# A Mamba-2 and mixture-of-experts layer: second modulation on TensorE column groups, residue products last, scan heads in turn on two array halves

## What is computed

```python
mx = modulation(c, ada_w, ada_b)              # silu(c) @ w + b, six vectors of 2048
hx = modulate(rms_norm(x, g0), mx[0], mx[1])  # the same for ctx with c_ctx
yx = ssd_mixer(hx, hc, ...)                   # two-direction Mamba-2 scan, context first
x = x + mx[2] * yx
hx = modulate(rms_norm(x, g1), mx[3], mx[4])
y = hier_moe(hx, ...)                         # top-1 group, top-2 of its experts
x = x + mx[5] * y
```

## Time and profile before

| | |
|---|---|
| median of 3 runs | 2401.31 us (2399.72 to 2412.43) |
| profiled execution, its own time | 2409.67 us |
| its span (first to last instruction) | 2408.1 us |
| PE busy, DVE busy, ACT busy | 85%, 50%, 20% of the span |
| mean clock of TensorE | 0.94 of full speed |

### The profile page before, as it was taken

How to read it: one execution, slowest core, us unless ns; L and a number is a source line. 1 busy time by engine, 2 the same in 40 slices (tenths; PEclk the granted TensorE clock), 3 DMA queues, 4 the chain that set the end, 5 groups by cost and what they waited for, 6 DMA issues and landing times. The chain is left out here.

```text
span 2408.1 us, 27833 instructions
## 1 busy us (share of the span) xinstructions
PE 2048.1 (85%) x9989; PEld 1254.5 (52%) x9989; DVE 1196.3 (50%) x1865; ACT 490.8 (20%) x513; POOL 107.0 (4%) x148
## 2 busy tenths in 40 slices
PE   4678999999999999996699769888888888888887
PEld 2257777777777777775478553333333333333332
DVE  2256776777777777776354553222222222222223
ACT  3122333333323233332244320000000000000000
POOL 0000000000000000000370000000000000000000
PEclk8678999999999999998899869999999999999999
DMA  6967656565647474646355509999999999999997
GB/s 223 318 198 215 180 160 189 155 202 146 211 132 225 127 214 142 212 146 223 117 188 195 222 35 379 422 422 422 422 422 422 422 421 422 422 422 422 422 422 309
DMA packets 296458, 660.42 MB, mean 274 GB/s; under 512 B 15968, under 2 KB 186400, under 8 KB 242016
## 3 DMA queue, kind: packets, MB, share of 16 engines
q1 hardware_dynamic: 288752, 635.30, 71.3%
q0 software_dynamic: 6672, 24.29, 2.8%
q10 hardware_dynamic: 992, 0.26, 0.1%
HBM read 653.32 MB, written 6.49 MB: 274 GB/s over the span
## 5 line engine op out<-in xcount | busy, mean ns | idle before, releaser
L1572 PE MATMUL bank<-wt,xe 128*64 128x512 f32 x2048 | 464.7, 596 | 111.3 <-DMA wt<-in_moe_w_up 108.2
L1377 PE MATMUL bank<-hTh,whi 128*128 128x256 f32 (+1 forms) x1280 | 450.3, 352 | 66.3 <-DVE wlo L867 45.3
L1378 PE MATMUL bank<-hTl,whi 128*128 128x256 f32 (+1 forms) x1280 | 441.0, 345 | 0.0
L1379 PE MATMUL bank<-hTh,wlo 128*128 128x256 f32 (+1 forms) x1280 | 440.8, 344 | 0.0
L1271 DVE TENSOR_TENSOR x<-x,bank 128x512 f32<-128x512 f32 x256 | 158.5, 681 | 544.5 <-PE bank L1559 544.5
L1572 PEld LDWEIGHTS bank<-wt,xe 128*64 128x64 f32 x2048 | 157.9, 137 | 412.2 <-issue 408.8
L1377 PEld LDWEIGHTS bank<-hTh,whi 128*128 128x128 f32 x1280 | 252.1, 197 | 114.2 <-issue 88.7
L1378 PEld LDWEIGHTS bank<-hTl,whi 128*128 128x128 f32 x1280 | 252.3, 197 | 25.6
L1379 PEld LDWEIGHTS bank<-hTh,wlo 128*128 128x128 f32 x1280 | 251.2, 196 | 27.1
L867 DVE TENSOR_TENSOR wlo<-raw,whi 128x2048 fp32r<-128x2048 f32 x81 | 185.3, 2287 | 92.8 <-ACT whi L645 88.5
L1597 PE MATMUL bank<-wt,hdn 128*64 128x512 f32 x1024 | 226.8, 596 | 1.4 <-DVE hdn L1283 1.4
(11 more groups left out here) (282 smaller groups left out, 1906.6 us busy)
## 6 DMA issues: line engine op xcount, KB each, us to landing
wt<-in_moe_w_gate SPq DMA_DIRECT2D x128, 1024.0 KB, 23.4
wt<-in_moe_w_up SPq DMA_DIRECT2D x128, 1024.0 KB, 25.5
wt<-in_moe_w_down SPq DMA_DIRECT2D x128, 1024.0 KB, 22.4
raw<-in_ada_w SPq DMA_DIRECT2D x96, 1024.0 KB, 5.3
raw<-in_ssm_w_in SPq DMA_DIRECT2D x81, 1024.0 KB, 5.9
raw<-in_ssm_w_out SPq DMA_DIRECT2D x32, 1024.0 KB, 4.9
bc<-cum_d POOLq DMA_DIRECT2D x32, 512.0 KB, 5.0
y_d<-ybuf POOLq DMA_DIRECT2D x32, 128.0 KB, 4.7
```

Of the source, the lines that this page charges most:

```text
L1377: pe.matmul(bank[:, 0:width], wh[:, k, :], hTh[:, k, 0:width], start=(k == 0), stop=False)
L1378: pe.matmul(bank[:, 0:width], wh[:, k, :], hTl[:, k, 0:width], start=False, stop=False)
L1379: last = pe.matmul(bank[:, 0:width], wl[:, k, :], hTh[:, k, 0:width], start=False, stop=(k == KC - 1))
L1572: last = pe.matmul(banks[0][SLOTS * h:SLOTS * h + SLOTS, :], xe[:, k, :], wt[2 * q + h][:, FF * i:FF * i + FF], start=(k == 0), stop=(k == ...
```

## The change

Three edits, and what hangs on them.

1. `ada_tile_sum` moves from DVE to PE. The four row chunks of a tile are multiplied with two columns of `cvec` on four column groups of the array (columns 0, 32, 64, 96), each into its own partitions of bank 2, four tiles to a sum. ACT copies the whole bank to `arow` (`ada_row`). PE adds the four groups with `sel`, which turns the row into columns at the same time (`ada_columns`, steps 4 and 9), and DVE adds them to the bias in place. The rows in DRAM, their way back, PE's transpose of them and their sum with the bias are gone. SP now frees a tile's slot by PE's semaphores `s_ada`.
2. `project` runs the 32 products with `whi` first and signals `s_wh`; then it waits for `s_lo` and runs the 16 with `wlo`. ACT waits for `s_wh` instead of `s_win`. The output projection follows the same idea: `yh` by `whi`, `yl` by `whi`, then `yh` by `wlo`, each with its own wait.
3. `y_chunk` no longer runs one head's six matmuls and then the other's. It gives the two heads turns, two instructions at a time, and each half signals its own semaphore `s_y[h]`.

The core of the diff:

```diff
@@ SP
                 else:
-                    sp.wait_ge(s_ada2, NADA * bg + (n + 1))
+                    for i in range(4):
+                        sp.wait_ge(s_ada[i], NADA * bg + (ADA1 + n + 1))
...
@@ ACT, conv_hi
                 if not (isinstance(g, int) and g == 0 and n == 0):
-                    act.wait_ge(s_win, m - 1)
+                    act.wait_ge(s_wh, m - 1)
...
@@ ACT, ada_row
-                act.wait_ge(s_asum, 2 * g + (j + 1))
-                act.activation(arow[0:1, :], ADAK[0:1, :], ACT.Copy).then_inc(s_adaev, 1)
-                act.wait_ge(s_adaev, 2 * g + (j + 1))
-                act.dma_start(mod2_d[bass.ds(2 * g + j, 1), :], arow[0:1, :]).then_inc(s_ads, 16)
+                for i in range(4):
+                    act.wait_ge(s_ada[i], NADA * g + (ADA1 + 4 * j + 4))
+                if not (isinstance(g, int) and g == 0 and j == 0):
+                    act.wait_ge(s_asum, 2 * g + j)
+                act.activation(arow[:, :], ADAK[:, :], ACT.Copy).then_inc(s_adaev, 1)
...
@@ DVE, steps
-                    if w and n in ADA_STEP:
-                        ada_tile_sum(g, ADA_STEP[n])
+                    if w and n == 5:
+                        ada_columns(g, 0)
                     if w:
                         drain(g, n)
+                    if w and n == 9:
+                        ada_columns(g, 1)
...
@@ DVE
+            def ada_columns(g, j):
+
+                dve.wait_ge(s_asum, 2 * g + (j + 1))
+                col = packs[:, 0, bass.ds(GROUPS * g + (ADA1 + 4 * j), 4)]
+                dve.tensor_tensor(col, ADAC[:, 8 * j:8 * j + 8:2], col, ALU.add).then_inc(s_ads, 1)
...
@@ PE, project
                 for k in range(KC):
                     pe.matmul(bank[:, 0:width], wh[:, k, :], hTh[:, k, 0:width], start=(k == 0), stop=False)
-                    pe.matmul(bank[:, 0:width], wh[:, k, :], hTl[:, k, 0:width], start=False, stop=False)
+                    last = pe.matmul(bank[:, 0:width], wh[:, k, :], hTl[:, k, 0:width], start=False, stop=False)
+                last.then_inc(s_wh, 1)
+                pe.wait_ge(s_lo, m + 1)
+                for k in range(KC):
                     last = pe.matmul(bank[:, 0:width], wl[:, k, :], hTh[:, k, 0:width], start=False, stop=(k == KC - 1))
                 last.then_inc(inc, 1)
...
@@ PE
+            def ada_tile_sum(g, j):
+
+                pos = POS[("a", j)]
+                pe.wait_ge(s_raw[raw_of(pos)], raw_count(group_raw(g), pos))
+                if j % 4 == 0:
+                    if isinstance(g, int) and g == 0 and j == 0:
+                        pe.wait_ge(s_azero, 1)
+                    else:
+                        pe.wait_ge(s_ads, 2 * g + j // 4)
+                for i in range(4):
+                    pe.matmul(ADAK[32 * i:32 * i + 2, :], cvec[:, 4 * (j % 4) + i, :], a_view(raw_of(pos))[:, i, :],
+                              start=(j % 4 == 0), stop=(j % 4 == 3), tile_position=(0, 32 * i)).then_inc(s_ada[i], 1)
+
+            def ada_columns(g, j):
+
+                pe.wait_ge(s_adaev, 2 * g + (j + 1))
+                for i in range(4):
+                    last = pe.matmul(ADAC[:, 8 * j + 2 * i:8 * j + 2 * i + 2], arow[:, P * i:P * i + P], sel[:, :], start=True, stop=True)
+                last.then_inc(s_asum, 1)
...
@@ PE, output projection
-                pe.wait_ge(s_yl, k + 1)
-                pe.wait_ge(s_lo, m + 1)
...
+                for ys_, seen, ring in ((yh, s_yh, whi), (yl, s_yl, whi), (yh, s_lo, wlo)):
+                    if ring is wlo:
+                        pe.wait_ge(s_lo, m + 1)
+                    else:
+                        pe.wait_ge(seen, k + 1)
+                        pe.wait_ge(s_hi, m + 1)
```

More of the change, by code:

```diff
@@ L266, in build @@
         s_win = sem("s_win")
+        s_wh = sem("s_wh")
         s_drain = sem("s_drain")
@@ L297, in build @@
         s_stev = sem("s_stev")
-        s_y = sem("s_y")
+        s_y = [sem(f"s_y{h}") for h in range(2)]
         s_fin1 = sem("s_fin1")
@@ L949, in differences @@
                 if hf == 1:
-                    dve.wait_ge(s_y, GC * s + 2)
+                    for h in range(2):
+                        dve.wait_ge(s_y[h], GC * s + 2)
                 for d in range(2):
@@ L993, in finish @@
             def finish(s, c):
-                dve.wait_ge(s_y, GC * s + (c + 1))
+                for h in range(2):
+                    dve.wait_ge(s_y[h], GC * s + (c + 1))
                 dve.wait_ge(s_dx, GC * s + (c + 1))
@@ L1423, in y_chunk @@
                     pe.wait_ge(s_fin1, GC * s + (c - 1))
[L1424 to L1434, removed]
-                            last = pe.matmul(o, xtok[:, 1, hs], wts[:, q, P:WC], start=False, stop=True)
-                last.then_inc(s_y, 1)
+                heads = []
+                for h in range(2):
+                    r = 2 * c + h
+                    heads.append((banks[6 + c % 2][64 * h:64 * h + 64, 0:L], slice(64 * r, 64 * r + 64), r % HALF))
+                for d in range(2):
+                    for o, hs, r in heads:
+                        pe.matmul(o, st[:, d, hs], ce[:, d * HALF + r, :], start=(d == 0), stop=False)
+                for o, hs, r in heads:
+                    pe.matmul(o, xdtf[:, 0, hs], wts[:, r, 0:2 * P], start=False, stop=False)
+                for o, hs, r in heads:
+                    pe.matmul(o[:, P:L], xdtf[:, 1, hs], wts[:, r, 2 * P:WC], start=False, stop=False)
+                for o, hs, r in heads:
+                    pe.matmul(o[:, 0:P], xtok[:, 0, hs], wts[:, HALF + r, 0:P], start=False, stop=False)
+                for h, (o, hs, r) in enumerate(heads):
+                    pe.matmul(o, xtok[:, 1, hs], wts[:, HALF + r, P:WC], start=False, stop=True).then_inc(s_y[h], 1)
             def c_times_b(g):
@@ L1473, in steps @@
                         c_times_b(g)
-                    if w and n in (3, 8):
-                        pe.wait_ge(s_acc, 32 * g + (16 if n == 3 else 32))
-                        pe.matmul(ADAK[0:1, :], ones[:, 0:1], arow[:, :], start=True, stop=True).then_inc(s_asum, 1)
+                    if w and n in ADA_STEP:
+                        ada_tile_sum(g, ADA_STEP[n])
+                    if w and n in (4, 9):
+                        ada_columns(g, n // 9)
             steps(0, True, False)
@@ L1496, in _ @@
                 m = M_OUT + k
-                pe.wait_ge(s_yl, k + 1)
-                pe.wait_ge(s_lo, m + 1)
-                for tt in range(TT):
-                    ys_, yls = yh[:, k, P * tt:P * tt + P], yl[:, k, P * tt:P * tt + P]
-                    for a, ring, first, final in ((ys_, whi, True, False), (ys_, wlo, False, False), (yls, whi, False, True)):
+                for ys_, seen, ring in ((yh, s_yh, whi), (yl, s_yl, whi), (yh, s_lo, wlo)):
[4 more added lines that the diff above has]
+                        pe.wait_ge(s_hi, m + 1)
+                    for tt in range(TT):
                         for nb in range(4):
-                            last = pe.matmul(banks[4 * tt + nb][:, :], a, ring[:, m % 2, 512 * nb:512 * nb + 512],
-                                             start=(k == 0 and first), stop=(k == IC - 1 and final))
+                            last = pe.matmul(banks[4 * tt + nb][:, :], ys_[:, k, P * tt:P * tt + P], ring[:, m % 2, 512 * nb:512 * nb + 512],
+                                             start=(k == 0 and ys_ is yh and ring is whi), stop=(k == IC - 1 and ring is wlo))
                 last.then_inc(s_wo, 1)
```

50 lines of the change are left out of this document (15 added, 35 removed).

## The result

| | median of the runs, us | to the kernel before |
|---|---|---|
| before | 2400.51 (2399.49 to 2412.43) | |
| after | 2377.16 (2375.63 to 2381.84) | 0.9894, 95% interval 0.9874 to 0.9914 |
| forecast | 2311 (2285 to 2352) | |

The change made the kernel 23 us faster, not 90, and the time lies above the range. The profiled execution took 2375.91 us, its span is 2374.4.

The account below looks back on a forecast made before the run. A round was taken as PE's own work plus some 15 us of DVE being late. Savings of 77 us in seven rounds, 5 in round 0 and 8 at the end gave 2320 for a profile, 2311 median (2285 to 2352).

Parts of the forecast that it names:

- DVE's small sums: DVE's additions of the finished modulation columns in the rounds: under 0.3 us each, placed behind the residues.
- the sum: All priced gains and costs: -77 us for seven rounds, -5 for round 0, -8 for half round and output projection.
- the second half's `weights`: In a round, DVE's `weights` for the second half end about 0.9 us after z2, a new wait.
- the 8.4 that I took off for the median: The last step: the median lay 8.4 us below the profiled execution, so 2320 for a profile became 2311.
- the 5.2 us: PE's hole before the x0 projection of a round, waiting for `wlo`; predicted to close wholly, gaining 5.2 us.
- the 4.6 us: Time a round loses to the lower clock around PE's holes; all 4.6 us taken as won.
- The rival in which the halves gain no more: Heads already overlap in part, so taking turns gains nothing: 41 us missing, 2352; chance 0.10.
- Tile sums and columns: New PE work a round: eight tile sums at 0.95 us, 7.6, and two `ada_columns` at 1.0, 2.0.
- The `raw` slots: Tile slots held until PE ends its step delay SP's loads: costed at nothing, at worst 16 us a round.
- The signs: Listed checks, among them rounds 111 us apart, clock above 0.98 and four heads in 4.4 us.
- what I had at -8: The half round's heads, a transpose and sum, and the output projection's earlier fourth chunk: together -8 us.
- the stall moves on: Late slots or ACT behind `decays` keep half the waiting and clock loss, 6.8 us a round: 2358; chance 0.14.

## Why the prediction was wrong

**The step that failed.** It is the sentence on DVE's small sums: they "stay under 0.3 each, behind the residues". Their length was right (0.16), their place was not looked up. I priced `ada_columns` as work on DVE and never as a wait: `pe.wait_ge(s_ads, 2 * g + j // 4)` stands in the diff, in `ada_tile_sum`, at j = 4, and nothing in the sum answers to it. The prediction held both numbers that it needed. It says that the second half's `weights` end 0.9 us after z2; tile 4 stands in front of z2 (6.0 us, and the tile 1.0) and waits for an operation behind `weights`: 0.9 + 6.0 + 1.0 = 7.9 us, measured 7.7. Times seven, with the lower clock behind it, that is the 59 us that the move of the columns gave back in the rounds.

**From the profile to the median.** The sum gave 2320 for a profile, and the changed kernel's was 2375.9: 56 us short, the 59 less a few in the stretches before and behind the rounds. The other part of the 66 us is the 8.4 that I took off for the median. They belonged to one profiled execution of the kernel before, which varies by more than that (2394 to 2415); after's median is 1.3 us above its profile. The version with the columns in step 4, 2321.0, has what the sum said for a profile. Its parts agree too: from the `dtw` transposes to the output projection its profile is 12.0 + 70.0 + 8.0 = 90 us below before's, where the sum has 87 and 3 more inside the output projection.

**The waits that were removed.** Their sizes held: no wait for `wlo` in the rounds, 0.45 us instead of 1.2 before the states, and, once the new wait is gone, 0.81 before the third chunk of heads where I had 0.9. Their cause did not: I wrote that the sums' move alone would not close the 5.2 us and that "the new order of `project` does". The sums' move closes it; the new order is worth 3 us.

**The clock.** Right as a rule of this kernel: 1.00 in the round of 111.2 us, where the longest wait is 0.81 us, and 0.80 behind the 7.7 us. I had taken all of the 4.6 us as won, and after has given back 1.6.

**The heads.** First and last rows of two chunks in PE's timeline of after, beside the earlier trace rows:

```profile
418.44 1.08 PE L1427 MATMUL bank<-ce,st 128*64 128x256 f32 x8
...
422.39 0.60 PE L1435 MATMUL bank<-wts,xtok 128*64 128x256 f32 x4
422.92 1.04 PE L1456 MATMUL bank<-raw,cvec 128*2 128x512 f32 x8
```

Four heads hold PE from 418.44 to 422.92, 4.5 us, worked out as 4.4. The rival in which the halves gain no more is refuted by the 42 us.

**Tile sums and columns.** 0.97 us a tile from start to start, forecast 0.95; 0.95 for the columns, forecast 1.0. After's page has all 64 tiles in one row, of which 54.1 of the idle 55.2 us are the new wait:

```profile
L1456 PE MATMUL bank<-raw,cvec 128*2 128x512 f32 x512 | 73.4, 647 | 55.2 <-DVE packs L1082 54.1
```

The Trainium skill, "TensorE: Matmul & The Clock Gate", section Part 3, would have put some 0.15 us on each tile for its increments. No run shows them: one and four took 0.97 us alike. Half of the front's 1.71 us, so its block at full clock, is 0.86; 0.11 us are left to 0.97. Whether the change to the four groups and back is in them isn't shown: in one group the same tile leaves as much, 3.53 - 8 x 0.427 = 0.11, with 0.427 as a quarter of the 1.71. The Trainium skill, "TensorEngine Tiling (Array Packing)", section Tiling Modes, says that such a change drains the array; if it does here, it costs at most these 0.11 us a tile.

**The `raw` slots.** Costed at nothing, and right: no wait of PE for a load in the rounds.

**The signs.** Two of those that I named showed that something was missing: rounds 119.7 us apart instead of 111, and a clock of 0.97 in them, not above 0.98. None of the three that were to prove the forecast wrong came (a tile sum over 1.3 us, four heads above 6, a wait for `whi` or for a tile): a wait for DVE's signal was not among them. Only the one tile a round right behind the hole takes over 1.3 us, 1.82 from start to start, and that by the low clock.

**The output projection.** PE's timeline in after:

```profile
1148.05 2.09 PE L1521 MATMUL bank<-whi,yh 128*128 128x512 f32 x8 [0.42 <-DVE a2row L1098]
...
1170.36 3.54 PE L1521 MATMUL bank<-whi,yh 128*128 128x512 f32 x8 [5.71 <-ACT whi L749]
```

It starts 32.4 us behind the last `states` instead of 41.0, and to the experts it is 2.2 us longer: -6.4 for what I had at -8. The 2.2 aren't the projection's. From its start to the first product behind it (L1528, before L1510) it takes 182.7 us instead of 184.4; the router's stage behind that takes 3.9 longer. The code there is the same, and its 64 products (L1543, before L1525) take 13.84 us at a granted clock of 0.50, where the profile of before had 10.61 at 0.67. The fourth chunk starts right behind its cast as forecast, but PE arrives there earlier too, since it no longer waits 3.06 us for a residue at the start. The hole stays at 5.7 because the load is late, and a load's lateness isn't won back by an earlier arrival of PE.

**The rivals.** None came true as told. The measured time is nearest to "the stall moves on" (2358 at a chance of 0.14), but it came by another path: I looked for the next late thing among casts and loads, the operands of PE, and not among the signals by which a bank comes free.

## What to carry to other kernels

Go through every wait that a diff adds, also those that only hand a bank back, and write beside each what stands ahead of the signalling instruction in its engine's queue. An operation of 0.16 us put behind 5.7 us of other work cost 59 us in seven rounds; moving it up by one step gave them back. And where an engine is late in a stretch, shorten its queue before reordering its consumer: a reordered consumer waits for the same queue one step later.

## What the runs showed of the hardware

- Four fp32 matmul pairs with two columns each, on four column groups, hold PE 0.97 us for what one group does in 3.53: 3.6 times as fast.
- Heads on alternate column halves run at full overlap: 4.5 us for 32 instructions of 256 columns and 16 of 128, where one head after the other took 7.0.
- The granted clock stays at 1.00 through waits of 0.45 and 0.81 us a round. Behind one of 7.7 us it is 0.50, so at 1.2 GHz, from 449.87 to 453.30 us, over the tile and the first products of z2. The cost is 1.6 us a round.
- Semaphore increments on four matmuls instead of one are not measurable (0.6 us of 2312, with single runs 2 to 3 us apart).
- Issuing four small loads (for the router, 2 to 256 KB) holds SP's queue for 12 us, and the load of 1 MB that stands behind them starts as late.
